# Two passes over the channels for the first four tiles of the first projection, with its modulation loaded in channel halves

## The chip, the cores and the metric

The kernel runs on one core of a Trainium2 chip. The metric is the device time of one execution in microseconds (us). All data are 32-bit floats. The engines of the core run their own instruction streams in order and meet at semaphores: TensorE (products and transposes into PSUM), VectorE, ScalarE and GpSimd (element work; GpSimd here mostly issues loads and stores), and SyncE, which only issues transfers. "Channels" are the 1024 columns of the model, in eight blocks of 128.

## The reference, cut to what matters

Two model blocks are computed one after the other on 1024 tokens of x and 256 context tokens. The change touches only the beginning, the modulated norm and the first product of the first layer:

```python
def _modulate(x, c, norm_g, w_ada, b_ada):      # its meaning, written short
    shift, scale, gate = split(silu(c) @ w_ada + b_ada, 3)   # 1024 columns each
    h = rmsnorm(x, norm_g) * (1 + scale) + shift
    return h, gate

h, gate = _modulate(x, c, ...)
hc, gate_c = _modulate(xc, c_ctx, ...)          # the context has its own condition
q, k, v, ... = _split(h @ w_in, ...)            # then rotation (rope) of q and k, attention, ...
```

The first 512 columns of `w_in` make the queries of the window attention; they are rotated and kept transposed. Everything behind that (attentions, a second layer, a state-space block, the embedding at the end) is not changed.

## The kernel before, in words

A planner in Python lays out the whole program as a list of stages. Every PSUM bank use is a numbered "fill" of a ring: `main` has banks 0 to 4, `turn` banks 5 and 6; bank 7 holds attention outputs later on. The writer of a fill waits until the bank's last fill was drained, the reader waits until the fill is full. Then each engine's program is written by one walk over the stages, so the order of work on each engine is this walk's order, and an engine that waits holds all that stands behind it.

The start of the program, before the change:

- SyncE (L850 to L865) loads, in this order, four chunks of the modulation weights (`ev_w_ada`, 512 columns each, 2 MB; chunks 0 and 1 are the shift, 2 and 3 the scale), the first projection weights (512 columns of `ev_w_in`, 2 MB), the rotation tables, the window mask, and the next projection's weights (1 MB).
- GpSimd (L882) loads tiles of x and the context (128 tokens, 0.5 MB) into three slots. From the fourth tile on it waits until a normed tile has left its slot: `gp.wait_ge(s_xn, j["xn"] - 2)`.
- ScalarE issues the small loads (L2249), makes the conditions, and then takes for each tile the sum of squares (L2188) and the inverse root (L2182, L2183).
- VectorE (L1858) multiplies each tile by its inverse root into one of seven slots of `RP`. After the fourth tile (`i == 3`) it does its part of the modulation: for each chunk a copy of the product out of PSUM (L1817) and, one chunk later, an addition of the bias (L1826), at the end the scale times the gain (L1833). After that come the even ones of the eight channel blocks of the first group of four tiles: the gain operation `hT = turned * scale + shift` (L1783). ScalarE does the odd ones (L2200) and waits for `s_mod` first.
- TensorE does all four chunks: `modulation` (L1208, sixteen instructions of products a chunk, four groups of rows side by side; L1218, eight small products that turn and sum them), then the transposes of the first group's eight blocks (L1135), then the first projection (L1318).

The first projection has ten tiles of 128 tokens. A tile is eight products of 128 x 512, issued as sixteen instructions, into one bank. Groups of normed tiles are turned between them: group 0 is tiles 0 to 3, group 1 tiles 4 to 7, group 2 the two context tiles 8 and 9. Group 1's eight blocks are turned after tiles 1 to 3 (three, three and two), group 2's after tiles 4 to 6. VectorE rotates a finished tile out of PSUM into one of three stage slots (`rope`: L1759, L1763, L1764, L1770), TensorE turns it (L1153) after the products of the following tile, and ScalarE copies it to `RQ` (L2237). `stage_free` makes VectorE wait until the tile three before was turned.

## Time and profile before

| what | value |
|---|---|
| median of 3 runs | 2816.3 us (2813.34 to 2818.73) |
| the profiled execution's own time | 2816.37 us |
| its span, first to last instruction | 2814.4 us |
| TensorE busy (products) | 2725.0 us, 97% of the span |
| VectorE, ScalarE, GpSimd busy | 1069.6, 785.2, 218.2 us |
| granted TensorE clock, mean | 0.994 of full |
| first projection product begins, last tile ends | 51.2 us, 139.0 us |

The profile is of one execution. Times in it are from the span's start. Line numbers (L1318) are those of the kernel before. "Wait before" of an instruction is the idle time of its engine ahead of it, with what released it. "psum<-RW,hT" names destination and sources by their buffers. PE is TensorE's products, PEld its weight loads, which may overlap products; DVE is VectorE, ACT ScalarE, POOL GpSimd, SP SyncE, and a q behind a name is that engine's issuing of transfers. Granted clock 1.00 is 2.4 GHz, 0.50 is 1.2 GHz.

### The profile page before, as it was taken

To read this page: it belongs to the slowest core of one execution; us is meant where nothing else is said; L and a number is where in the kernel's file an instruction comes from. 1 tells how busy PE (TensorE), PEld (TensorE's weight loads), DVE (VectorE), ACT (ScalarE), POOL (GpSimd) and SP (SyncE) were. 2 spreads that over 40 slices of the span, in tenths; PEclk is the share of its full clock that TensorE was granted. 3 is DMA by queue.
4 is the path that set the end of the run, shared out by engine and by line. 5 is a ranking of instruction groups with operands and counts; after the bars stand their busy time and mean duration, and the time that the engine had idled before them with its cause. 6 is when DMAs were issued, how large, how long until landed. Compare 5 with 4: busy or idle time off the path is not lost.

```text
span 2814.4 us, 32462 instructions
## 1 busy us (share of the span) xinstructions
PE 2725.0 (97%) x12154; PEld 1528.1 (54%) x12154; DVE 1069.6 (38%) x3023; ACT 785.2 (28%) x1684; POOL 218.2 (8%) x401
## 2 busy tenths in 40 slices
PE   5999999999999999999999999999999999999999
PEld 2477544477744445466655476444564465644444
DVE  3257521199811233344400075123744373412211
ACT  3136400177711112222200165112211363121100
POOL 2000000000000000000060030010000002011000
PEclk8999999999999999999999999999999999999999
DMA  7031000012012220211011101152220104125321
GB/s 262 4 104 41 20 30 30 30 68 72 20 53 74 90 86 27 94 38 38 12 34 40 40 24 39 64 97 90 108 102 30 68 17 133 68 92 185 131 75 49
DMA packets 73019, 188.46 MB, mean 67 GB/s; under 512 B 6972, under 2 KB 9728, under 8 KB 71936
## 3 DMA queue, kind: packets, MB, share of 16 engines
q0 software_dynamic: 26656, 94.84, 10.5%
q1 hardware_dynamic: 45456, 91.16, 9.4%
q8 instruction: 99, 1.62, 0.3%
q14 instruction: 56, 0.46, 0.1%
q10 hardware_dynamic: 752, 0.38, 0.0%
HBM read 143.69 MB, written 43.01 MB: 66 GB/s over the span
## 4 chain that ended last, share of the span: by engine, by line
PE 92%; DVE 3%; issue 2%; ACT 2%; DMA 1%; ACTq 0%; POOL 0%; DVEq 0%
PE psum L1318 32%; PE psum L1282 13%; PE psum L1354 11%; PE psum L1366 6%; PE psum L1297 5%; PE psum L1384 5%; PE psum L1450 4%; PE psum L1381 4%; PE psum L1518 4%; PE psum L1153 1%; PE psum L1503 1%; PE psum L1523 1%; PE psum L1135 1%; PE psum L1208 1%; PE psum L1488 1%
## 5 line engine op out<-in xcount | busy, mean ns | idle before, releaser
L1318 PE MATMUL psum<-RW,hT 128*128 128x512 f32 (+2 forms) x2208 | 923.8, 573 | 7.5 <-ACT hT L2200 4.7
L1318 PEld LDWEIGHTS psum<-RW,hT 128*128 128x128 f32 x2208 | 427.1, 197 | 433.2 <-issue 411.3
L1282 PE MATMUL psum<-RW,RQ 128*128 128x512 f32 x832 | 360.9, 592 | 1.1 <-ACT RQ L2237 1.1
L1354 PE MATMUL psum<-RQ 64*128 64x256 f32 (+5 forms) x1344 | 291.7, 492 | 2.3 <-DVE small L2041 1.5
L2390 ACT ACTIVATE RP<-RP,small 128x1280 f32<-128x1280 f32 (+11 forms) x274 | 251.9, 920 | 131.1 <-DVE small L2041 127.0
L2041 DVE CUSTOM_DVE_ANT_0 RP<-psum,small 128x512 f32<-128x512 f32 (+1 forms) x382 | 201.4, 573 | 178.5 <-PE psum L1354 89.7
L1282 PEld LDWEIGHTS psum<-RW,RQ 128*128 128x128 f32 x832 | 156.3, 190 | 189.3 <-issue 189.3
L1366 PE MATMUL psum<-ident,RP 128*128 128x128 f32 x1388 | 203.7, 281 | 9.8 <-DVE RP L2054 4.5
L2402 ACT ACTIVATE RP<-psum 128x512 f32<-128x512 f32 (+1 forms) x288 | 149.9, 521 | 192.2 <-PE psum L1366 180.4
L1366 PEld LDWEIGHTS psum<-ident,RP 128*128 128x128 f32 x1388 | 149.3, 141 | 81.7 <-issue 67.9
L1354 PEld LDWEIGHTS psum<-RQ 64*128 64x128 f32 (+1 forms) x1344 | 139.2, 186 | 90.4 <-issue 48.9
L1384 PE MATMUL psum<-RQ,RP 128*128 128x128 f32 x1312 | 159.8, 276 | 0.5 <-ACT YR L2412 0.5
L1384 PEld LDWEIGHTS psum<-RQ,RP 128*128 128x128 f32 x1312 | 152.1, 192 | 5.3 <-issue 4.6
L2054 DVE COPY RP<-psum 128x512 f32<-128x512 f32 (+1 forms) x160 | 109.2, 682 | 75.0 <-PE psum L1366 73.9
L1381 PE MATMUL psum<-RP,RQ 128*64 128x128 f32 x1856 | 124.3, 278 | 1.6 <-DVE RP L2054 1.5
L1297 PE MATMUL psum<-hT,RW 128*128 128x512 f32 (+1 forms) x320 | 123.8, 550 | 0.0
L1518 PE MATMUL psum<-RW,hT 128*128 128x512 f32 x256 | 114.2, 599 | 2.7 <-DMA RW<-in_w_ple_gate 2.7
L1381 PEld LDWEIGHTS psum<-RP,RQ 128*64 128x64 f32 x1856 | 99.3, 136 | 26.9 <-issue 26.5
L1450 PE MATMUL psum<-RW,hT 128*128 128x512 f32 x256 | 111.7, 594 | 0.0
L2188 ACT ACTIVATE RP<-RX 128x1024 f32<-128x1024 f32 x44 | 46.4, 1054 | 192.6 <-DVE small L1729 164.6
L1297 PEld LDWEIGHTS psum<-hT,RW 128*128 128x128 f32 x320 | 60.7, 190 | 62.8 <-issue 61.2
L2237 ACT ACTIVATE RQ<-psum 128x512 f32<-128x512 f32 (+1 forms) x53 | 29.4, 555 | 231.8 <-PE psum L1153 231.8
(320 smaller groups left out, 2282.1 us busy)
## 6 DMA issues: line engine op xcount, KB each, us to landing
RW<-in_w_in SPq DMA_DIRECT2D x7, 2048.0 KB, 7.9
RW<-in_ev_w_in SPq DMA_DIRECT2D x6, 2048.0 KB, 7.9
RW<-in_od_w_ada SPq DMA_DIRECT2D x6, 2048.0 KB, 8.0
RW<-in_od_w_in SPq DMA_DIRECT2D x5, 2048.0 KB, 7.9
RQ<-in_ev_w_ada SPq DMA_DIRECT2D x4, 2048.0 KB, 21.0
RX<-in_x POOLq DMA_DIRECT2D x16, 512.0 KB, 6.0
y_even<-YR POOLq DMA_DIRECT2D x20, 256.0 KB, 2.3
RP<-y_even POOLq DMA_DIRECT2D x20, 256.0 KB, 3.0
```

Of the source, the lines that this page charges most:

```text
L1282: last = pe.matmul(main.bank(f), yT[:, kk, :], w_buf(n)[:, kk, :], start=kk == 0, stop=kk == KC - 1)
L1297: last = pe.matmul(main.bank(e["m"])[:, 0:e["n"]], w_buf(n)[:, kk, e["c0"]:e["c0"] + P], src[:, kk, e["t0"]:e["t0"] + e["n"]], start=kk == ...
L1318: last = pe.matmul(main.bank(f)[:, 0:nc_], lhs_of(st["lhs"], j["t"], kk), w, start=kk == 0, stop=kk == kn - 1)
L1354: last = pe.matmul(main.bank(f)[:, 0:pc["w"]], q, kk[:, keys], start=i == 0, stop=i == len(u["qk"]) - 1)
L1366: last = pe.transpose(turn.bank(ch["f"])[:, i * P:(i + 1) * P], pair_slot(st, u, lane)[:, at:at + P], ident[:, :])
L1381: last = pe.matmul(bank_o[64 * lane:64 * lane + 64, 0:P], u["v"][:, kt, vc:vc + 64], p_t, start=first, stop=final)
L1384: last = pe.matmul(bank_o[:, P * lane:P * lane + P], p_t, u["v"][:, kt, vc:vc + P], start=first, stop=final)
L1450: last = pe.matmul(main.bank(e["m"]), lhs_of("h", e["t"], kk), w_buf(e["w"])[:, kk, :], start=kk == 0, stop=kk == KC - 1)
L1518: last = pe.matmul(main.bank(fg), hT3[:, kk, tok], w_buf(st["w"][c])[:, kk, :], start=kk == 0, stop=kk == KC - 1)
L2041: drained(main, dve.tensor_tensor_reduce(pair_slot(st, u, lane)[:, pc["at"]:pc["at"] + pc["w"]], main.bank(f)[:, 0:pc["w"]], add, -scale, ...
L2390: fn(pr, pr, ACT.Exp, bias=mins[:, at, lane, n - 1:n], scale=-1.0, accum_out=sums[:, at, lane:lane + 1]).then_inc(s_pexp, 1)
L2402: turn.consumed(fn(pair_turned(ch["c"])[:, 0:n], turn.bank(ch["f"])[:, 0:n], ACT.Copy), ch["f"])
```

## The change

1. The modulation weights load in the order of columns 0, 2, 1, 3: shift and scale of the lower 512 channels first, then those of the upper 512. The first projection's weights are loaded in two pieces of four channel blocks: the lower piece between the second and the third chunk, the upper piece behind the fourth.
2. A new ring `early` has bank 7 alone. Each chunk of modulation (`first_modulation`) uses it twice, for its products and for the turned sum, which now follows in the same call; its reader is VectorE in both.
3. x tile 3 is loaded into `gate[:, 0:1024]`, which is not yet in use, without waiting for a slot. Tile 4 of x waits for the fourth modulation chunk's weights to land.
4. TensorE does chunks 0 and 1, two turned blocks, then the products over channel blocks 0 to 3 of tiles 0 to 3 into four banks; chunk 2 comes after tile 1, chunk 3 after tile 3. Then the upper four blocks of tiles 0 to 3 are added. Turned blocks of group 0 stand between tile 0's products.
5. Group 1's blocks are turned four after tile 2 and four after tile 3. A rotated tile is turned later than before: tile 0 after tile 3, 1 after 4, 2 and 3 after 5, 4 and 5 after 6, 6 to 8 after 7 to 9 (before: each tile after the next one's products).
6. VectorE makes the scales in halves and norms tiles 4 to 7 after all of group 0; tile 8 after the rotation of tile 0, tile 9 after group 1's first four blocks. ScalarE takes the square sums of tiles 4 to 8 after group 0's blocks.

The core of the diff, on the planner's side and the engines' new functions:

```diff
-        for _ in range(5):
-            plan_ada_chunk(even_cols)
+        for j in (0, 2, 1, 3):
+            n = new_weights(kview(ada_w[:, j * 512:(j + 1) * 512]), KC, 512, slot=2 + j)
+            even_cols["w"].append(n)
+            even_cols["steps"].append({"n": n, "j": j, "fill": early.new("dve"), "turned": early.new("dve")})
         stages += [even_cols, plan_norm(with_ctx, 0, True)]
-        gs = stages[-1]["groups"]
-        turns_a = planned([(1, gs[1], 3), (2, gs[1], 3), (3, gs[1], 2), (4, gs[2], 3), (5, gs[2], 3), (6, gs[2], 2)])
+        first_norm, gs = stages[-1], stages[-1]["groups"]
+        def plan_first(src, tiles, dst):
+            n = new_weights(src, KC, 512)
+            r = {"kind": "rope", "w": n, "dst": dst, "turns": 4, "lhs": "h", "gain": None, "back": False}
+            jobs = planned([(2, gs[1], 4), (3, gs[1], 4), (4, gs[2], 3), (5, gs[2], 3), (6, gs[2], 2)])
+            now = {3: [0], 4: [1], 5: [2, 3], 6: [4, 5], 7: [6], 8: [7], 9: [8]}
+            r["tiles"] = [{"t": t, "m": main.new("dve"), "hook": None, "jobs": jobs.get(t, []), "now": now.get(t, []),
+                           "needs": {4: gs[1], 8: gs[2]}.get(t)} for t in tiles]
+            for j in r["tiles"]:
+                if j["t"] < 4:
+                    number_turns(j["jobs"])
+                for i in j["now"] + ([9] if j["t"] == 9 else []):
+                    r["tiles"][i]["f"] = turn.new("act")
+                    r["tiles"][i]["st"] = new_stage(r["tiles"][i]["f"])
+                if j["t"] >= 4:
+                    number_turns(j["jobs"])
+            weights[n]["last"] = r["tiles"][-1]["m"]
+            return r
...
+        first_proj = plan_first(kview(we[:, 0:512]), with_ctx, qaT)
+        stages += [first_proj,
...
+            return gate[:, 0:1024] if i == 3 else RX[:, (i % 3) * 1024:(i % 3 + 1) * 1024]
...
+                if n == even_cols["w"][2]:
+                    f = first_proj["w"]
+                    sp.dma_start(w_buf(f)[:, 0:4, :], weights[f]["src"][:, 0:4, :]).then_inc(s_half, 16)
+                if n == first_proj["w"]:
+                    sp.dma_start(w_buf(n)[:, 4:KC, :], w["src"][:, 4:KC, :]).then_inc(s_w[w["slot"]], 16)
+                else:
+                    sp.dma_start(w_buf(n), w["src"]).then_inc(s_w[w["slot"]], 16)
...
-                        if j["x"] >= 3:
+                        if t == 4:
+                            wait_weights(gp, even_cols["w"][3])
+                        if j["x"] > 3:
                             gp.wait_ge(s_xn, j["xn"] - 2)
...
+            def first_modulation(c):
+                step = even_cols["steps"][c]
+                n, f = step["n"], step["fill"]
+                wait_weights(pe, n)
+                main.wait_drained(pe, f_cond)
+                early.wait_free(pe, f)
+                for r in range(2):
+                    for g in range(4):
+                        kk = 4 * r + g
+                        last = pe.matmul(early.bank(f)[32 * g:32 * g + 32, :], cond3[:, kk, :], w_buf(n)[:, kk, :],
+                                         start=r == 0, stop=r == 1)
+                early.written(last)
+                early.wait_drained(pe, f)
+                f = step["turned"]
+                for b in range(4):
+                    last = pe.matmul(early.bank(f)[:, 2 * b:2 * b + 2], mod_part(c)[:, b * P:(b + 1) * P], select3[:, :, 0],
+                                     start=True, stop=True)
+                early.written(last)
+            def first_projection(st):
+                n = st["w"]
+                g0 = first_norm["groups"][0]
+                def products(j, ks):
+                    f = j["m"]
+                    for kk in ks:
+                        if j["t"] == 0:
+                            turn.wait_drained(pe, g0["fills"][kk])
+                        last = pe.matmul(main.bank(f), lhs_of("h", j["t"], kk), w_buf(n)[:, kk, :], start=kk == 0, stop=kk == KC - 1)
+                        if j["t"] == 0 and kk + 2 in ks:
+                            turn_groups([(g0, kk + 2)])
+                    return last
+                turn_groups([(g0, 0), (g0, 1)])
+                pe.wait_ge(s_half, 16)
+                for j in st["tiles"][:4]:
+                    main.wait_free(pe, j["m"])
+                    products(j, range(4))
+                    if j["t"] == 0:
+                        turn_groups([(g0, 4), (g0, 5)])
+                    if j["t"] == 1:
+                        first_modulation(2)
+                first_modulation(3)
+                wait_weights(pe, n)
+                for j in st["tiles"]:
+                    if j["t"] < 4:
+                        main.written(products(j, range(4, KC)))
+                        turn_groups(j["jobs"])
+                    else:
+                        if j["needs"]:
+                            wait_group(j["needs"])
+                        main.wait_free(pe, j["m"])
+                        main.written(products(j, range(KC)))
+                    for i in j["now"]:
+                        turn_stage(st, st["tiles"][i])
+                    if j["t"] >= 4:
+                        turn_groups(j["jobs"])
...
-                    for i, j in enumerate(st["tiles"]):
-                        dve.wait_ge(s_rstd, j["rq"] + 1)
-                        if j["xn"] >= 7:
-                            turn.wait_full(dve, xn_group[j["xn"] - 7])
-                        sig(ts(xn_slot(j["xn"]), x_slot(j["x"]), rstd[:, j["rq"] % 8, 0:1], None, ALU.mult), s_xn)
-                        if i == 3:
-
-                            for c in range(len(even_cols["steps"])):
-                                modulation(even_cols, c)
-                            normed_groups(st["jobs"])
+                    for j in st["tiles"][:4]:
+                        norm_tile(j)
+                    first_modulation(0)
+                    first_modulation(1)
+                    first_scales(0)
+                    normed_groups(st["jobs"][:4])
+                    first_modulation(2)
+                    first_modulation(3)
+                    first_scales(1)
+                    mark(s_mod)
+                    mods[0] += 1
+                    dve.wait_ge(s_mod, mods[0])
+                    normed_groups(st["jobs"][4:])
+                    for j in st["tiles"][4:8]:
+                        norm_tile(j)
...
+                elif st is first_proj:
+                    for j in st["tiles"]:
+                        f, t = j["m"], j["t"]
+                        if t == 3:
+                            normed_groups(j["jobs"])
+                        main.wait_full(dve, f)
+                        stage_free(j["st"])
+                        so = stage_slot(j["st"])
+                        if t < NT:
+                            sig(rope(main.bank(f), 8, so, t, f), s_stage)
+                        else:
+                            drained(main, dve.tensor_copy(so, main.bank(f)), f)
+                            mark(s_stage)
+                        if t == 0:
+                            norm_tile(first_norm["tiles"][8])
+                        if t != 3:
+                            normed_groups(j["jobs"])
+                        if t == 2:
+                            norm_tile(first_norm["tiles"][9])
...
+                    for j in st["tiles"][:4]:
+                        norm_tile(j)
+                    for half in range(2):
+                        act.wait_ge(s_scale, half + 1)
+                        normed_groups(st["jobs"][4 * half:4 * half + 4])
+                    for j in st["tiles"][4:9]:
+                        norm_tile(j)
+                elif st is first_proj:
+                    for j in st["tiles"]:
+                        if j["t"] < 4:
+                            normed_groups(j["jobs"])
+                        if j["t"] == 2:
+                            norm_tile(first_norm["tiles"][9])
+                        for i in j["now"]:
+                            turned(st, st["tiles"][i])
+                        if j["t"] >= 4:
+                            normed_groups(j["jobs"])
+                    unturned = (st, st["tiles"][-1])
```

## Rows read from the trace of the kernel before

**Rows 1.** The page: shares of the chain that ended last, by engine
```profile
PE 92%; DVE 3%; issue 2%; ACT 2%; DMA 1%; ACTq 0%; POOL 0%; DVEq 0%
```

**Rows 2.** The chain, 0 to 150 us: start, length, what held it
```profile
8.09 8.73 DMA YR<-in_ev_b_lambda
...
20.84 6.62 DMA RX<-in_x
...
29.98 0.61 DVE RS L1817
30.63 1.87 PE psum L1218 x8
32.49 3.57 PE psum L1208 x16
...
44.13 0.82 DVE hT L1783
45.00 0.92 PE psum L1135 x4
...
79.95 6.87 PE psum L1318 x16
```

**Rows 3.** DMA issues, 0 to 120 us; the last number is us to landing
```profile
RW<-in_ev_w_in SPq DMA_DIRECT2D x1, 2048.0 KB, 24.9
```

**Rows 4.** Timeline, TensorE and SyncE's queue: start, length (us), operation, wait before it
```profile
16.27 5.19 SPq L861 DMA_DIRECT2D RW<-in_ev_w_in  x1
...
19.81 0.15 PEld L1208 LDWEIGHTS psum<-RQ,cond 128*32 128x32 f32 x4 [1.05 <-DMA RQ<-in_ev_w_ada]
...
51.22 13.97 PE L1318 MATMUL psum<-RW,hT 128*128 128x512 f32 x32 [0.92 <-ACT hT L2200]
...
89.76 7.11 PE L1318 MATMUL psum<-RW,hT 128*128 128x512 f32 x16 [1.16 <-ACT hT L2200]
...
99.77 7.03 PE L1318 MATMUL psum<-RW,hT 128*128 128x512 f32 x16
...
108.66 7.03 PE L1318 MATMUL psum<-RW,hT 128*128 128x512 f32 x16
...
117.09 7.03 PE L1318 MATMUL psum<-RW,hT 128*128 128x512 f32 x16
...
124.39 7.03 PE L1318 MATMUL psum<-RW,hT 128*128 128x512 f32 x16
```

**Rows 5.** Windows: busy us of PE, PEld, DVE, ACT, POOL; granted clock; DMA
```profile
30.00:41.00 11.00, 10.37 (x48) 4.74 (x48) 2.20 (x5) 0.00 (x0) 0.53 (x1) 0.50 1.05 391
...
45.50:48.50 3.00, 2.95 (x14) 2.32 (x12) 1.35 (x2) 0.78 (x1) 0.00 (x0) 0.50 0.01 5
```

**Rows 6.** Timeline of VectorE: modulation end, norms of tiles, rotations
```profile
43.57 0.17 DVE L1826 TENSOR_TENSOR small<-psum,small 128x8 f32<-128x8 f32 x1 [0.72 <-PE psum L1218]
...
59.06 0.88 DVE L1858 TENSOR_SCALAR RP<-RX,small 128x1024 f32<-128x1024 f32 x1 [2.36 <-ACT small L2183]
...
64.94 0.69 DVE L1759 TENSOR_TENSOR RS<-psum,cos_t 128x512 f32<-128x512 f32 x1
...
69.11 0.80 DVE L1783 TENSOR_SCALAR hT<-psum,small 128x512 f32<-128x512 f32 x1
```

**Rows 7.** Timeline of ScalarE: square sums of x tiles
```profile
18.07 1.04 ACT L2188 ACTIVATE RP<-RX 128x1024 f32<-128x1024 f32 x1
...
19.67 1.04 ACT L2188 ACTIVATE RP<-RX 128x1024 f32<-128x1024 f32 x1
...
57.32 1.06 ACT L2188 ACTIVATE RP<-RX 128x1024 f32<-128x1024 f32 x1 [1.40 <-DMA RX<-in_x]
```

**Rows 8.** Timeline of GpSimd: the load of x tile 7
```profile
53.80 0.53 POOL L882 DMA_DIRECT2D RX<-in_x  x1 [23.00 <-DVE RP L1858]
```

**Rows 9.** Timeline of TensorE: later modulation products at the full clock
```profile
206.24 1.92 PE L1208 MATMUL psum<-RW,cond 128*32 128x512 f32 x16
...
613.13 1.05 PE L1218 MATMUL psum<-select,RS 128*128 128x2 f32 x8
```

More of the change, by code:

```diff
@@ L170, in build @@
         turn = Ring(psum, [5, 6], sem("turn_full"), {"act": sem("turn_read_act"), "dve": sem("turn_read_dve")})
+        early = Ring(psum, [7], sem("first_modulation_full"), {"dve": sem("first_modulation_read")})
         s_first = sem("conditions_loaded")
+        s_scale = sem("first_scales_ready")
+        s_half = sem("first_input_weights_half_loaded")
+        s_x3 = sem("x_row_tile3_loaded")
         s_rows = sem("vectors_loaded")
@@ L715, in x_slot, with wait_x @@
         def x_slot(i):
-            return RX[:, (i % 3) * 1024:(i % 3 + 1) * 1024]
+            return gate[:, 0:1024] if i == 3 else RX[:, (i % 3) * 1024:(i % 3 + 1) * 1024]
+        def wait_x(eng, i):
+            if i == 3:
+                eng.wait_ge(s_x3, 16)
+            else:
+                eng.wait_ge(s_x[i % 3], 16 * (i // 3 + 1) - (16 if i % 3 == 0 and i > 3 else 0))
         def stage_slot(i):
@@ L853, in _ @@
                 if w["before"] is not None:
-                    main.wait_full(sp, weights[w["before"]]["last"])
+                    (early if w["before"] in even_cols["w"] else main).wait_full(sp, weights[w["before"]]["last"])
                 if n == even_rows["w"][0]:
@@ L1235, in _ @@
                 if k == "ada":
-                    for c in range(len(st["steps"])):
-                        modulation(st, c)
+                    first_modulation(0)
+                    first_modulation(1)
                 elif k == "norm":
-                    turn_groups(st["jobs"])
+                    continue
+                elif st is first_proj:
+                    first_projection(st)
+                    unturned = (st, st["tiles"][-1])
+                    later += [(turn, j["f"]) for j in st["tiles"][-2:]] + [(main, st["tiles"][-1]["m"])]
                 elif k in ("gated", "final", "plain"):
@@ L1847, in modulation, with norm_tile, first_modulation, first_scales @@
                 dve.wait_ge(s_mod, mods[0])
+            def norm_tile(j):
+                dve.wait_ge(s_rstd, j["rq"] + 1)
+                if j["xn"] >= 7:
+                    turn.wait_full(dve, xn_group[j["xn"] - 7])
+                sig(ts(xn_slot(j["xn"]), x_slot(j["x"]), rstd[:, j["rq"] % 8, 0:1], None, ALU.mult), s_xn)
+            def first_modulation(c):
+                step = even_cols["steps"][c]
+                f, j = step["fill"], step["j"]
+                early.wait_full(dve, f)
+                drained(early, dve.tensor_copy(mod_part(c), early.bank(f)), f)
+                f = step["turned"]
+                early.wait_full(dve, f)
+                drained(early, tt(modc[:, 4 * j:4 * j + 4, :], early.bank(f)[:, 0:8].rearrange("p (b j) -> p b j", j=2),
+                                  bada[0][:, 4 * j:4 * j + 4].unsqueeze(2).broadcast_to([P, 4, 2]), ALU.add), f)
+            def first_scales(half):
+                fence()
+                ks = slice(4 * half, 4 * half + 4)
+                for j in range(2):
+                    last = stt(sclc[:, j, ks], modc[:, 8 + 4 * half:12 + 4 * half, j], 1.0, ngain[0][:, ks], ALU.add, ALU.mult)
+                sig(last, s_scale)
+                fence()
             y_g = [0]
@@ L1892, in _ @@
                         if c == 0:
-                            dve.wait_ge(s_x[j["x"] % 3], 16 * (j["x"] // 3 + 1))
+                            wait_x(dve, j["x"])
                         main.wait_full(dve, f)
@@ L2238, in turned, with norm_tile @@
                 turn.consumed(last, f)
+            def norm_tile(j):
+                wait_x(act, j["x"])
+                square_sum(x_slot(j["x"]), j["xn"], j["rq"])
+                inverse_rms(j["rq"], 1, 1.0 / D)
             sq_index = {}
@@ L2285, in _ @@
                 if k == "norm":
-                    for i, j in enumerate(st["tiles"]):
-                        act.wait_ge(s_x[j["x"] % 3], 16 * (j["x"] // 3 + 1))
-                        square_sum(x_slot(j["x"]), j["xn"], j["rq"])
-                        inverse_rms(j["rq"], 1, 1.0 / D)
-                        if i == 3:
-                            act.wait_ge(s_mod, 1)
-                            normed_groups(st["jobs"])
+                    for j in st["tiles"][:4]:
[5 more added lines that the diff above has]
+                        norm_tile(j)
+                elif st is first_proj:
+                    for j in st["tiles"]:
[7 more added lines that the diff above has]
+                            normed_groups(j["jobs"])
+                    unturned = (st, st["tiles"][-1])
                 elif k in ("gated", "final", "plain"):
```

10 lines of the change are left out of this document (5 added, 5 removed).

## The prediction

> **What bounds the kernel now.** The page comes first: TensorE carries 92% of the chain of waits [rows 1], so a saving counts only where TensorE waits or works late. Then the chain of the first 150 us [rows 2]: before 51 us it does not run on projection work at all. It goes over a slow constant load (until 16.8 us), a load of x that waited for a free slot (20.8 to 27.5), and then link by link over copy, eight small products and sixteen modulation products. The reader should see two things there. The load of x tile 3 is the only one that holds the modulation up: VectorE takes the modulation only after it has normed tile 3. And the first projection weights, issued at 16.3 us, landed 24.9 us later, at 41.2 [rows 3, 4], ten us ahead of their first use at 51.22 [rows 4]. From 51.22 on TensorE's own rows tell the rest: tile 4 begins at 89.76, tiles 5 to 8 at 99.77, 108.66, 117.09 and 124.39 [rows 4]. A tile is 6.87 us [rows 2] and one turn of a rotated tile 0.43 (7.30 from tile 7 to tile 8), so what is above that is turns of normed tiles and waits. Last the clock: granted 0.50 (1.2 of 2.4 GHz) from 30 to 41 us, behind a wait of 8 us and although TensorE was busy 10.4 of these 11 us, and 0.50 once more from 45.5 to 48.5 [rows 5].
>
> I follow one moment through the change: the start of tile 4, before at 89.76.
>
> **Start, and the first two modulation chunks.** Tile 3 of x gets a slot of its own (in gate) and loads at once, so the load of 6.6 us leaves the chain. ScalarE starts at 18.07 and takes 1.60 us a tile [rows 7]; 1.74 us after the start of a tile VectorE can norm it, for 0.75 [rows 6, 7]. Tile 3 is then normed at 18.07 + 3 x 1.60 + 1.74 + 0.75 = 25.4 instead of 29.98 [rows 2]. The constants that let ScalarE and TensorE begin came last at 16.8 [rows 2], on a queue that now shares with 0.5 MB more. I add 0.6 (bounds 0, if the order of packets does not change, and 2.2, a third of the x load of 6.6 us). So 26.0.
> Modulation now runs through one bank, so chunk 1 cannot multiply before VectorE has read chunk 0's turned values. Chunk 0's products, 3.57 from 16.8 on, lie under the norming. What is left: copy 0.65, small products 1.87, read 0.2, products 3.57, copy with its signals 0.8, small products 1.87 [rows 2], together 9.0: 35.0. The weights for it are no wait, since TensorE's weight load for the second chunk was released by its landing at 19.81 [rows 4]; with 0.5 MB more of x beside it, some 1.3 us later (as 2 MB took 5 to 6).
> Four transposes at the low clock, 0.92, and one gain operation, 0.82 [rows 2], put the first channel block at 36.8. Projection so begins 14.4 us earlier than 51.22. Its lower weight half is 1 MB behind two chunks and lands well before.
>
> **The two passes.** PE's work is not reduced, only cut: four half tiles are 4 x 3.43 = 13.7, four groups of transposes 1.8, and two modulation chunks stand between them. At the full clock the sixteen products are 1.85 (1.92 in the row, less its overlap) and the eight small ones 1.0 [rows 9], with a wait of 0.9 for VectorE's copy between them that nothing covers, because TensorE is in order: 3.8 a chunk, 7.5 for two. The clock is low at the start. The two low stretches of before that TensorE worked through lasted 3 us and 11 us [rows 5], which costs half of each, 1.5 to 5.5; I take 2.6, nearer to the short one, since 512-column products without a gap follow. Sum: 36.8 + 13.7 + 1.8 + 7.5 + 2.6 = 62.4. Call this moment X: the last modulation product.
>
> **After X, the part that decides.** VectorE adds the bias and makes the second scales (0.56 before, 43.57 to 44.13 [rows 2, 6], now with two more waits on itself: 0.9), then the gain operation 0.8: TensorE starts the upper pass at X + 1.75. Tile 0 with the turns of blocks 6 and 7 between its products ends at X + 6.2, tiles 1 and 2 at X + 9.6 and X + 13.05.
> Norming of tiles 4 to 7 is behind all this on both engines. ScalarE ends block 7 at X + 5.3 and starts x tile 4; VectorE norms it from X + 7.0; only then may GpSimd ask for x tile 7, whose slot is tile 4's (1.05 us after the norm began: its 0.75, and 0.3 that I allow for the signal). From issue to ScalarE's start were 3.52 (53.80 to 57.32 [rows 7, 8]), so X + 11.5, and tile 7 is normed at 11.5 + 1.74 + 0.75 = X + 14.0. TensorE waits there for 1 us: the next transposes need all four tiles.
> It turns blocks 0 and 1 of tiles 4 to 7, and there it stands. Two turn banks; block 2 needs block 0 drained; VectorE drains even blocks, and its order is norm 7, rotation of tile 0, norm of tile 8, rotations of tiles 1 and 2, and only then block 0. Two rotations in a row, from the first one's start to a gain operation, are 4.17 (64.94 to 69.11 [rows 6]). So 14.15 + 2.15 + 0.85 + 4.17 = X + 21.3, plus 0.8 for the block: X + 22.1, while TensorE had finished block 1 at X + 15.0. **This new wait of 7.1 us is the change's main cost.** Behind it on TensorE are the upper pass of tile 3, blocks 4 to 7 and tile 0's deferred turn.
> From X + 22.15: two groups of transposes 0.9, half a tile 3.43, blocks 4 to 7 with the bank waits 2.95 (four times 0.44, and twice 0.6 of a gain operation that the banks expose), tile 0's turn with its wait 1.05. After 7 us of idling I expect the clock low again, with the same bounds and the same value, 2.6. So 22.15 + 0.9 + 3.43 + 2.95 + 1.05 + 2.6 = 33.1, less 0.5 because waits for a gain operation overlap the slow transposes: X + 32.6 = 95.0, against 89.76: **+5.2**.
>
> **From tile 4 to the end of the projection.** The products are the same. After tile 4 the deferred turn comes as soon as before, but VectorE's rotation must wait for it to free a stage slot: +0.45. After tile 5 two rotated tiles are turned (0.43 more) and one more block with its bank wait: gap 2.6 against 108.66 - 99.77 - 6.87 = 2.0. After tile 6 2.05 against 1.56. Tiles 7 to 9 as before. Sum **+1.5**. All later stages keep their order, TensorE nearly fills them, and their weights are released by this projection's last tile, so I carry the shift to the end unchanged: +6.7 on the profiled execution's 2816.4, which is the median of the runs shown (2816.3): **2823 us**.
> No price: the extra descriptors on SyncE's queue (one more issue, on a queue that is free of work from there to the last tile), x tiles 4 to 6 loading after 34 instead of at 20 (used after X + 5), the tables, needed at X + 14. If that cover went, the first would delay weights that have ten us in hand.
>
> **Rivals.** (a) The clock falls at each modulation gap too. TensorE there does bursts of 1.85 and 1.0 with 0.9 idle; for it speaks that 45.5 to 48.5 was low soon after sixteen small products and short waits [rows 5], against it that the long low stretch stood behind a whole wait of 8 us, and the gaps here are 0.9. Two low stretches of 3.3 us cost 1.7 each: 2826.5.
> The Trainium skill, page "TensorE: Matmul & The Clock Gate", section "A second HAM failure mode: psum-queue depth-cycling", states that short idles between groups of products make the clock gate swing and that bursts then pay the re-throttling; by that rule rival (a) would hold. The trace agrees in part, with its 0.50 at 45.5 to 48.5.
> (b) The clock stays high wherever I let it fall (the early stretch shorter, none after the stall): -2.6 and up to -1: 2819.5. For the first, the short stretch of [rows 5]; against the second, the only wait of that length in these rows ended at 0.50.
> (c) Faster: VectorE is not late. If x tile 7 came so early, or the rotations lay so well beside the upper passes, that block 0 was drained as it was turned, the 7.1 us and the low clock behind them (2.6) and the 1 us at X + 14 fall away: tile 4 at 84.3, 2812.3. It decides at X + 15: only a VectorE that has done three rotations by then wins, and rotation 2 can't begin before tile 2 ends at X + 13.05. For more than 0.2% the waits ahead of X would have to shrink too; TensorE's bare work from 35 to tile 4 is 41 us, so 2804 is the floor.
> (d) The change does not start projection early, because the constants or chunks land late: each us there is one us at the end; 2 us more give 2825.
>
> **How the numbers follow.** 0.2%, 5.6 us, is about what can be told from no change. Forecast, 2820 to 2826: 0.45. (a) with (d), 2824 to 2831: 0.22. (b), 2816 to 2820: 0.23. (c), 2804 to 2813: 0.10. The range 2814 to 2830 leaves out (c) and the end of (a). Slower than 2821.9: two thirds of the forecast case and nearly all of (a), 0.52; faster than 2810.7: 0.06; the rest, 0.42, is no change.
>
> **What the profile after would show.** Right: projection products from about 37 us; modulation products between them at about 48 and 59; then TensorE idle some 7 us between two groups of transposes of RP, released by VectorE's hT, shortly before 85, and the clock 0.50 behind it; tile 4 at 93 to 97. Wrong: no idle of over 3 us there, or tile 4 before 89; or modulation chunks in the gap of 3.6 us each (rival a). What would make it wrong most easily is the position of X, into which four terms go that are only bounded.

## The result, and the profile after

The changed kernel takes 2825.4 us (median of 5 runs, 2823.8 to 2829.6), the kernel before 2814.4 (5 runs, 2813.3 to 2818.7): ratio 1.0039, with a 95% interval of 1.0028 to 1.0051, slower by 11 us. The profiled execution took 2823.8 us, its span is 2821.6, and 7.2 us of span lie between the two profiles.

TensorE's timeline of the changed kernel: start, length, line, operation, and in brackets the wait before. L1294 is the product line of the first projection, L1275 the modulation's products, L1281 its small products, L1174 the transposes of normed tiles. A row with x8 or x16 is that many instructions in a line; eight instructions of 512 columns are half a tile.

```profile
17.96 3.64 PE L1275 MATMUL psum<-RQ,cond 128*32 128x512 f32 x16 [4.17 <-DMA YR<-in_ev_b_lambda]
...
29.32 3.27 PE L1275 MATMUL psum<-RQ,cond 128*32 128x512 f32 x16 [0.35 <-DVE small L1966]
...
36.01 2.05 PE L1294 MATMUL psum<-RW,hT 128*128 128x512 f32 x2 [0.63 <-DVE hT L1885]
...
46.50 1.92 PE L1275 MATMUL psum<-RQ,cond 128*32 128x512 f32 x16
49.24 1.05 PE L1281 MATMUL psum<-select,RS 128*128 128x2 f32 x8 [0.81 <-DVE RS L1963]
...
59.93 1.05 PE L1281 MATMUL psum<-select,RS 128*128 128x2 f32 x8 [0.81 <-DVE RS L1963]
62.65 1.90 PE L1294 MATMUL psum<-RW,hT 128*128 128x512 f32 x2 [1.66 <-DVE hT L1885]
...
67.00 9.02 PE L1294 MATMUL psum<-RW,hT 128*128 128x512 f32 x20
76.87 1.09 PE L1174 MATMUL psum<-ident,RP 128*128 128x128 f32 x8 [0.84 <-DVE RP L1956]
84.97 1.97 PE L1174 MATMUL psum<-ident,RP 128*128 128x128 f32 x8 [7.01 <-DVE hT L1885]
86.73 5.28 PE L1294 MATMUL psum<-RW,hT 128*128 128x512 f32 x8
...
95.47 7.03 PE L1294 MATMUL psum<-RW,hT 128*128 128x512 f32 x16
...
105.62 0.44 PE L1174 MATMUL psum<-ident,RP 128*128 128x128 f32 x2 [1.55 <-DVE hT L1885]
...
146.26 3.62 PE L1420 MATMUL psum<-RW,hT 128*128 128x256 f32 x16
```

Read it against [rows 4]. Projection begins at 36.0 instead of 51.2. Modulation chunks 2 and 3 stand between the half tiles (their small products at 49.24 and 59.93), each with a wait of 0.81 in its middle. The row at 84.97 is the result in one line: TensorE had turned two blocks of group 1 by 77.96, and the next transposes waited 7.01 us for a VectorE operation that writes hT. Tile 4 begins at 95.47, against 89.76 in [rows 4], and the next projection (L1420) at 146.26, against 139.0 in the table ahead.

VectorE in that wait (L1956 norms a tile, L1861 begins a rotation, L1885 is the gain operation):

```profile
69.61 0.75 DVE L1956 TENSOR_SCALAR RP<-RX,small 128x1024 f32<-128x1024 f32 x1 [3.36 <-ACT small L2336]
...
75.92 0.89 DVE L1956 TENSOR_SCALAR RP<-RX,small 128x1024 f32<-128x1024 f32 x1 [2.36 <-ACT small L2336]
76.94 0.69 DVE L1861 TENSOR_TENSOR RS<-psum,cos_t 128x512 f32<-128x512 f32 x1
...
78.94 0.89 DVE L1956 TENSOR_SCALAR RP<-RX,small 128x1024 f32<-128x1024 f32 x1
79.93 0.69 DVE L1861 TENSOR_TENSOR RS<-psum,cos_t 128x512 f32<-128x512 f32 x1
...
82.11 0.69 DVE L1861 TENSOR_TENSOR RS<-psum,cos_t 128x512 f32<-128x512 f32 x1
...
84.11 0.80 DVE L1885 TENSOR_SCALAR hT<-psum,small 128x512 f32<-128x512 f32 x1
```

Norm of tile 7, rotation of tile 0, norm of tile 8, rotations of tiles 1 and 2, and at 84.11 block 0, which TensorE had turned at 77.

The granted clock of some stretches (the number ahead of the DMA's two):

```profile
26.00:32.00 6.00, 4.55 (x24) 2.45 (x24) 1.21 (x3) 0.00 (x0) 0.00 (x0) 0.50 1.05 387
44.00:62.00 18.00, 15.36 (x70) 6.43 (x69) 2.32 (x8) 0.51 (x1) 0.00 (x0) 1.00 0.06 19
62.00:66.00 4.00, 3.35 (x7) 1.78 (x8) 1.06 (x2) 0.27 (x1) 0.00 (x0) 0.60 0.00 0
84.00:90.00 6.00, 5.03 (x12) 3.11 (x13) 2.34 (x4) 2.31 (x5) 1.39 (x3) 0.50 0.09 11
```

The clock is at 0.50 as the second chunk is multiplied (26 to 32; the first one, at 17.96, took 3.64 us as well), at full level through both modulation gaps (44 to 62), low again as the upper pass begins, and low for six us behind the long wait, where half a tile takes 5.28 us instead of the 3.60 that the same eight instructions take at full level below.

### The profile page after: what moved, and what is told of

It is laid out like the page before. It is cut to its first block, busy times and chain, and to the rows that moved or that the text cites. A ratio compares the mean times of both kernels' runs of the same rounds, so it can differ in the third digit from the quotient of the medians.

```text
span 2821.6 us, 32467 instructions
## 1 busy us (share of the span) xinstructions
PE 2727.2 (97%) x12154; PEld 1529.0 (54%) x12154; DVE 1070.2 (38%) x3026; ACT 785.4 (28%) x1684; POOL 218.8 (8%) x401
## 4 chain that ended last, share of the span: by engine, by line
PE 92%; DVE 3%; issue 2%; ACT 2%; DMA 1%; ACTq 0%; POOL 0%; DVEq 0%
PE psum L1420 30%; PE psum L1384 13%; PE psum L1456 11%; PE psum L1468 6%; PE psum L1399 5%; PE psum L1486 5%; PE psum L1552 4%; PE psum L1483 4%; PE psum L1620 4%; PE psum L1294 2%; PE psum L1192 1%; PE psum L1605 1%; PE psum L1625 1%; PE psum L1174 1%; PE psum L1590 1%
## 5 line engine op out<-in xcount | busy, mean ns | idle before, releaser
L1420 PE MATMUL psum<-RW,hT 128*128 128x512 f32 (+2 forms) x2048 | 855.0, 573 | 5.4 <-ACT hT L2353 2.6
L1420 PEld LDWEIGHTS psum<-RW,hT 128*128 128x128 f32 x2048 | 398.0, 198 | 397.6 <-issue 377.0
```

Source lines behind the costliest of these rows:

```text
L1420: last = pe.matmul(main.bank(f)[:, 0:nc_], lhs_of(st["lhs"], j["t"], kk), w, start=kk == 0, stop=kk == kn - 1)
```

## The experiments

For each the start of tile 4 in its profile is compared, and the interval from the first product of the projection to tile 4, because the first product itself moves between executions of one kernel (36.0 in the profile above, 37.9 in the next one). The changed kernel has 59.5 us from the first product to tile 4, and 60.1 in its second profile: differences of half a us between single profiles mean nothing.

**The changed kernel again.** No edit.

> The changed kernel once more, unaltered. The profiled executions stood 7.4 us apart, the medians 11. If the forecast's terms are all there is, tile 4 begins at 95 to 96 us again and the median lies 7 to 8 us above before (ratio 1.0026). If something later in the program also costs, the ratio stays near 1.0039 and the shift between the two profiles grows behind the first projection.

2827.6 us, ratio 1.0041 (1.0028 to 1.0055): the ratio stays, as the second case of the expectation has it. Tile 4 begins at 97.95, 60.1 us behind the first product; the wait for the gain operation is 7.00. The start is 2 us later than in the first profile. Behind the projection 2.5 us more are lost: from the start of the next projection (146.26 and 148.75) to the end the first profile takes 2675.3 us and this one 2677.9. The two profiles part at 1130 to 1160, where the granted clock of the three stretches of 10 us is 0.83, 0.88 and 0.78 here and 0.94, 1.00 and 1.00 there. A low stretch near 2230 to 2244 stands in both profiles and tells nothing of their difference; more on it below. So the wait is a constant of the program, the clock is not.

**Blocks ahead of the rotations.**

```diff
                         f, t = j["m"], j["t"]
-                        if t == 3:
-                            normed_groups(j["jobs"])
+                        if t < 2:
+                            normed_groups(st["tiles"][t + 2]["jobs"])
                         main.wait_full(dve, f)
...
-                        if t != 3:
+                        if t > 3:
                             normed_groups(j["jobs"])
```

> VectorE takes the gain operations of group 1's first four blocks ahead of the rotation of tile 0 and those of the other four ahead of the rotation of tile 1. Theory A (VectorE's order makes the 7 us wait, and the low clock stands behind it): the wait of 7.0 us shrinks to under 1, no stretch at clock 0.50 between 80 and 91, tile 4 begins at 86 to 87 instead of 95.5, time 8 to 9 us below the changed kernel, 2816. Theory B (the two passes and the modulation gaps inside them cost, and TensorE would be held somewhere else): tile 4 begins no earlier than 92, time at most 3 us below the changed kernel.

```profile
80.75 1.26 PE L1174 MATMUL psum<-ident,RP 128*128 128x128 f32 x8 [0.54 <-DVE hT L1885]
81.84 3.60 PE L1294 MATMUL psum<-RW,hT 128*128 128x512 f32 x8
...
88.90 7.03 PE L1294 MATMUL psum<-RW,hT 128*128 128x512 f32 x16
```

The wait is 0.54, half a tile behind it 3.60, and tile 4 begins 50.8 us behind the first product: 8.6 us less than in the changed kernel. 2819.9 us, ratio 1.0017 (1.0008 to 1.0026), 5.5 us below the changed kernel's median. The local gain is as expected. The total falls short of it, where 8 to 9 us were expected: this profile has a low stretch at 99 to 108 (tile 5 takes 8.7 us) and starts 2 us late, but whether that is so in the other ten runs, no profile shows. The same 8.73 us for tile 5 stand in two more profiles below (the slot of its own, the spread modulation) and not in the rest.

**x tile 7 in a slot of its own.**

```diff
-            return gate[:, 0:1024] if i == 3 else RX[:, (i % 3) * 1024:(i % 3 + 1) * 1024]
+            if i in (3, 7):
+                return gate[:, 0:1024] if i == 3 else gate[:, 1024:2048]
+            return RX[:, (i % 3) * 1024:(i % 3 + 1) * 1024]
...
-                        if j["x"] > 3:
+                        if j["x"] > 3 and j["x"] != 7:
                             gp.wait_ge(s_xn, j["xn"] - 2)
```

> The changed kernel with x tile 7 in a slot of its own too, so that its load no longer waits for the norm of tile 4. Theory A (the order on VectorE makes the wait): the norm of tile 7 comes 1.5 us earlier, but then tile 8 is waited for, and the three rotations still stand ahead of block 0: the wait before block 2 stays at 7 to 7.5 us, tile 4 begins at 94.5 to 95, under 1 us gained. Rival (the late load of x tile 7 is the cause): the wait falls under 3 us.

```profile
77.67 1.04 PE L1179 MATMUL psum<-ident,RP 128*128 128x128 f32 x8
85.33 1.97 PE L1179 MATMUL psum<-ident,RP 128*128 128x128 f32 x8 [6.63 <-DVE hT L1890]
...
94.89 7.03 PE L1299 MATMUL psum<-RW,hT 128*128 128x512 f32 x16
```

The wait is still 6.63, a little less than the 7 to 7.5 expected. The late load of x tile 7 is not its cause. First product to tile 4 is 57.1 us, 2.3 less than in the changed kernel, where under 1 was expected: 0.8 of it is the wait at 76 that is gone, 1 us a shorter low stretch behind the long wait (half a tile in 4.33 instead of 5.28), 0.4 the wait itself. One execution, 2824.9 us.

**The kernel before with x tile 3 in its own slot, alone.**

```diff
-            return RX[:, (i % 3) * 1024:(i % 3 + 1) * 1024]
+            return gate[:, 0:1024] if i == 3 else RX[:, (i % 3) * 1024:(i % 3 + 1) * 1024]
...
-                        if j["x"] >= 3:
+                        if j["x"] > 3:
                             gp.wait_ge(s_xn, j["xn"] - 2)
```

> The kernel before with one part of the change alone: x tile 3 in a slot of its own. Theory (that load was the only thing that held the modulation): VectorE takes the modulation at about 26 to 27 us instead of 29.98, chunks and transposes follow, first product at 47 to 48 instead of 51.2, time 3 to 4 us below before. Rival (the loads of weights, later by 0.5 MB, take its place): first product within 1 us of 51.2, no gain.

```profile
27.17 1.22 PE L1226 MATMUL psum<-select,RS 128*128 128x2 f32 x8 [4.01 <-DVE RS L1825]
...
35.59 3.64 PE L1216 MATMUL psum<-RQ,cond 128*32 128x512 f32 x16 [2.90 <-DMA RQ<-in_ev_w_ada]
...
51.03 13.97 PE L1326 MATMUL psum<-RW,hT 128*128 128x512 f32 x32 [0.92 <-ACT hT L2208]
```

VectorE does take the modulation 3.5 us earlier (27.17 against 30.63 in [rows 2]), but then TensorE waits 2.90 us for a modulation chunk to land, and the first product comes at 51.03. 2816.4 us, ratio 1.0005 (0.9996 to 1.0014). The rival was right in the time, which gains nothing that the runs can tell, and in that behind the load of x tile 3 stood the fourth chunk, at 35.6. "Within 1 us of 51.2" holds only against the first profile of before, whose clock was higher: here it is 0.50 from 36 to 48. The third profile of before, below, has the same clock there and begins the fourth chunk at 37.78 and its first product at 53.20, so of the 3.5 us some 2.2 are left like with like. The changed kernel does not meet this wait: between 17.96 and 36.01 its TensorE waits for VectorE alone, since two chunks and half of the projection's weights are enough for it to begin.

**Norms of tiles 4 to 6 in the idle time.**

```diff
                     normed_groups(st["jobs"][:4])
+                    for j in st["tiles"][4:7]:
+                        norm_tile(j)
                     first_modulation(2)
...
-                    for j in st["tiles"][4:8]:
-                        norm_tile(j)
+                    norm_tile(st["tiles"][7])
```

The same on ScalarE, between the two halves of the scales.

> The changed kernel with the square sums and norms of x tiles 4 to 6 done right behind the first four gain operations, where ScalarE and VectorE are idle (41 to 61 us), so that x tile 7 is loaded early too; the rotations still stand ahead of block 0. Theory A: VectorE begins the rotations 6 us earlier, as soon as tile 0 is complete, the wait before block 2 shrinks from 7.0 to about 2.5 us (rotation 2 can only start when tile 2 is complete), tile 4 begins at 89 to 91, time 5 to 7 us below the changed kernel. If instead the order alone counts and not when VectorE starts, the wait stays at 7.

```profile
79.12 1.09 PE L1174 MATMUL psum<-ident,RP 128*128 128x128 f32 x8 [2.02 <-DVE hT L1885]
80.05 5.29 PE L1294 MATMUL psum<-RW,hT 128*128 128x512 f32 x8
...
88.80 7.03 PE L1294 MATMUL psum<-RW,hT 128*128 128x512 f32 x16
```

The wait is 2.02, where about 2.5 was expected; 52.6 us from the first product to tile 4, 6.8 less than in the changed kernel, though the half tile behind even this wait took 5.29. 2819.8 us, ratio 1.0015 (1.0006 to 1.0024).

**Both: early norms, and blocks 0 to 3 ahead of the rotation of tile 2.**

```diff
-                        if t == 3:
+                        if t in (2, 3):
                             normed_groups(j["jobs"])
...
-                        if t != 3:
+                        if t > 3:
                             normed_groups(j["jobs"])
```

> The early norms of x tiles 4 to 6, and in addition VectorE takes blocks 0 to 3 of group 1 ahead of the rotation of tile 2 and the other four ahead of that of tile 3. Theory A: the 2.0 us that were left of the wait and the low clock behind it go too, tile 4 begins at 85 to 86, 10 us ahead of the changed kernel; the next projection 3 us ahead of before.

```profile
78.07 1.09 PE L1174 MATMUL psum<-ident,RP 128*128 128x128 f32 x8 [0.47 <-DVE hT L1885]
78.99 3.60 PE L1294 MATMUL psum<-RW,hT 128*128 128x512 f32 x8
...
86.05 7.03 PE L1294 MATMUL psum<-RW,hT 128*128 128x512 f32 x16
```

Wait 0.47, no low clock behind it, 49.6 us to tile 4. The next projection begins at 136.84, 2.2 us ahead of the first profile of before (3 expected). 2815.5 us, ratio 1.0003 (0.9994 to 1.0013): the order on VectorE and ScalarE alone brings the changed kernel back to where before is.

**The modulation spread out, nothing else.**

```diff
                     if j["t"] == 0:
                         turn_groups([(g0, 4), (g0, 5)])
+                        first_modulation(2)
                     if j["t"] == 1:
-                        first_modulation(2)
-                first_modulation(3)
+                        first_turned(2)
+                        first_modulation(3)
+                    if j["t"] == 2:
+                        first_turned(3)
```

`first_turned` is the second half of `first_modulation`, called from there for chunks 0 and 1.

> The changed kernel with nothing moved on VectorE or ScalarE; only TensorE's modulation is spread out: products of chunk 2 after tile 0's lower half, their turn after tile 1, products of chunk 3 right behind, their turn after tile 2, so that copies and scales lie under products. Theory B's share: two waits of 0.8 us, the 1.7 us before the upper pass and the low clock at 62 to 66 go, 4.5 us in all, while the wait of 7 us stays: tile 4 at 90.5 to 91.5. If theory A were all, tile 4 would stay at 94 to 96.

```profile
54.00 3.70 PE L1300 MATMUL psum<-RW,hT 128*128 128x512 f32 x8
...
58.35 4.54 PE L1300 MATMUL psum<-RW,hT 128*128 128x512 f32 x10
...
82.24 1.97 PE L1174 MATMUL psum<-ident,RP 128*128 128x128 f32 x8 [7.03 <-DVE hT L1894]
...
92.11 7.03 PE L1300 MATMUL psum<-RW,hT 128*128 128x512 f32 x16
```

No wait over 0.4 us is left between the half tiles and before the upper pass, and no low clock there (tile 0's upper half runs on at 58.35). The wait for VectorE is 7.03, untouched. 54.2 us to tile 4: 5.3 less than in the changed kernel, where 4.5 was expected; 0.6 of it is a shorter low stretch behind the long wait (half a tile in 4.65 instead of 5.28). Tile 4's own time, 92.1, is above the 90.5 to 91.5 expected because this execution began its products at 38.0. 2821.3 us, ratio 1.0020 (1.0011 to 1.0029).

**All three together.** The edits of the last two.

> Early norms, blocks ahead of the rotations and the spread-out modulation together. Both shares add: tile 4 begins at 80 to 82 instead of 95.5 (before 89.8), next projection 7 to 8 us ahead of before, time 2806 to 2809, ratio to before 0.9975. If the shares cover the same time, tile 4 begins at 84 to 86 and the gain over before is 3 us.

```profile
72.56 1.10 PE L1174 MATMUL psum<-ident,RP 128*128 128x128 f32 x8 [0.47 <-DVE hT L1894]
...
80.55 7.03 PE L1300 MATMUL psum<-RW,hT 128*128 128x512 f32 x16
...
131.34 3.62 PE L1429 MATMUL psum<-RW,hT 128*128 128x256 f32 x16
```

The shares add: 44.4 us from the first product to tile 4 is 15.0 less than in the changed kernel, against a sum of 15.2 (9.9 from the early norms with the blocks ahead, 59.5 to 49.6, and 5.3 from the spread modulation). The next projection begins at 131.34, 7.7 us ahead of the first profile of before. 2811.9 us, ratio 0.9986 (0.9977 to 0.9994): faster, but by 2 us in the median and 4 by the ratio, where 2806 to 2809 us and a ratio of 0.9975 were expected. The profiled execution, 2809.96 us, was the second fastest of its eleven.

**The context tiles' blocks ahead of their rotations too.**

```diff
-                        if t in (2, 3):
+                        if t >= 2:
                             normed_groups(j["jobs"])
...
-                        if t > 3:
-                            normed_groups(j["jobs"])
```

> The version with everything together, and in addition VectorE takes the context tiles' blocks ahead of the rotations of tiles 4 to 6. Theory: the wait of 1.56 us after tile 4 (for a gain operation that stands behind a rotation) falls to 0.5, nothing else moves much: the next projection begins 1 to 1.5 us earlier than in that version (131.3), time 1 us below it.

```profile
83.06 7.03 PE L1300 MATMUL psum<-RW,hT 128*128 128x512 f32 x16
...
91.22 0.66 PE L1174 MATMUL psum<-ident,RP 128*128 128x128 f32 x4 [0.47 <-ACT RQ L2398]
91.72 7.03 PE L1300 MATMUL psum<-RW,hT 128*128 128x512 f32 x16
```

From tile 4 to tile 5 are 8.66 us (10.42 in the version before this one). This is the best version: 2809.2 us, ratio 0.9974 (0.9964 to 0.9984), in the median 5 us below the kernel before and 16 below the changed one. From the first product to the next projection are 94.2 us, 1.0 less than in the version before, as expected; that the median is 2.8 us lower, where 1 was expected, the two intervals, which overlap, don't bear out. The profiled execution took 2812.6, the slowest of its nine, with the first product at 37.9.

**The kernel before with 6.9 us of products that nobody reads.** It adds work and changes no order.

```diff
+                        if st is stages[2] and j["t"] == 3:
+                            for kk in range(kn):
+                                pe.matmul(psum[:, 7, 0:nc_], lhs_of("h", j["t"], kk), w_buf(n)[:, kk, :],
+                                          start=kk == 0, stop=kk == kn - 1)
```

> The kernel before with eight more products behind tile 3 of the first projection, into a bank that nobody reads: 6.9 us of pure shift at full clock, no order and no wait changed. In every altered kernel so far the ratio lies 2 to 4 us above what its profile shows at the end of the first projection. Theory S (the level of the clock in the sparse stages behind depends on when they come, so that any shift away from before costs some 3 us more): ratio 1.0034 to 1.0038. Theory T (a shift is worth itself, and the rest belongs to the changed code): ratio 1.0024.

2821.1 us, ratio 1.0021 (1.0013 to 1.0030). Theory T: 6.9 us cost 6 (by the ratio) to 7 us (in the median), the 1.0034 of theory S lies outside the interval, and a later start of what follows carries no price of its own.

**Two more profiles of the kernel before.** No edit.

> The kernel before once more, for a second profile. If the stretches at clock 0.50 behind the first projection are a matter of the single execution, this one has them at other places than the first (1130 to 1150 and 2670), or of another length, and none or one near 2230.

> The kernel before a third time. Its first profile had tile 4 at 89.8 us, its second at 86.7, because the clock rose 6 us earlier in the modulation. If the early one is the usual case, it is 86.7 here too and the time under 2815; if the two levels are equally common, either may show, and the median of before lies between.

The second profile of before, then the third (L1218 are the modulation's small products, and the 7.1 us rows start tile 4):

```profile
35.78 1.05 PE L1218 MATMUL psum<-select,RS 128*128 128x2 f32 x8
36.76 1.92 PE L1208 MATMUL psum<-RQ,cond 128*32 128x512 f32 x16
...
86.72 7.10 PE L1318 MATMUL psum<-RW,hT 128*128 128x512 f32 x16 [1.16 <-ACT hT L2200]
```

```profile
35.99 1.87 PE L1218 MATMUL psum<-select,RS 128*128 128x2 f32 x8
37.78 3.64 PE L1208 MATMUL psum<-RQ,cond 128*32 128x512 f32 x16
...
91.53 7.10 PE L1318 MATMUL psum<-RW,hT 128*128 128x512 f32 x16 [1.17 <-ACT hT L2200]
```

and the granted clock of the same six us in both:

```profile
36.00:42.00 6.00, 5.50 (x48) 3.81 (x47) 2.87 (x8) 0.41 (x1) 0.00 (x0) 1.00 1.05 384
```

```profile
36.00:42.00 6.00, 6.00 (x31) 3.00 (x28) 1.36 (x3) 0.00 (x0) 0.00 (x0) 0.50 1.06 386
```

One program, the same instructions, and tile 4 at 86.7, 89.8 (the first profile) or 91.5. The own times of the three executions are 2813.3, 2816.4 and 2818.1 us, in the same order and as far apart. Both expectations held in part. What differs most from one execution to the next is the start, and the early case is not the only usual one. Behind the projection the low stretches of the three stand mostly at the same places, against what was expected: each has one within 1130 to 1150 and within 2670 to 2690 (0.91 or 0.83 on the mean of 20 us), only the second has one at 1840 to 1860 (0.91), and none has one near 2230.

That last place is where the changed order differs. Before, then the changed kernel:

```profile
2220.00:2250.00 30.00, 25.57 (x194) 14.45 (x193) 20.40 (x83) 16.53 (x63) 1.09 (x2) 1.00 0.26 89
```

```profile
2220.00:2250.00 30.00, 27.06 (x144) 13.99 (x142) 15.01 (x66) 12.55 (x50) 0.55 (x1) 0.83 0.22 79
```

The granted clock of these 30 us is 1.00 in all five profiles with the order of before (the two with an edit too) and 0.83 to 0.94 in eight of the nine with the changed order; only the one with all three edits has 1.00. From one and the same VectorE instruction near 2220 to another near 2250 it is 29.3 us in each of the five and 30.3 to 31.7 in the eight, so 1 to 2.4 us are lost. Why the clock falls there was not tested. It is made up for elsewhere in most executions: from the start of the next projection to the end, eleven of the fourteen profiles take 2675.0 to 2675.5 us, whichever order they have, and three of the changed order more (2676.4 with all three edits, 2677.9 the changed kernel again, 2678.3 with the context tiles' blocks ahead).

## Why the prediction was right, and where its size was off

The direction, and the mechanism with its place, were right, and 2825.4 lies in the range. Step by step:

- **Start.** The products of the projection were to begin at 36.8 and began at 36.0. The constants came 1.1 us later than before (17.96 against 16.8), for which 0.6 was allowed; with x tile 3's slot as the only change they come at 18.02, and at 16.77 to 17.04 in the four profiles that load it as before, so its load is what delays them. In nine profiles with the changed start the first product stands at 36.0 to 36.5 four times and at 37.8 to 38.1 five times, and 36.8 lies between. That the load of x tile 3 was "the only one" that held the modulation up was wrong: taken alone, its removal leads to a wait of 2.9 us for the fourth chunk, and no gain in time that the runs can tell. The forecast for the changed kernel did not hang on this, since there the chunks come in another order.
- **The two passes.** X came at 61.0, forecast 62.4. A modulation chunk was 3.65 us (3.8), with the wait of 0.81 (0.9). Rival (a), the clock falling at each gap, held neither at the first gap nor, if one reads the stretch at 1.00 from 44 to 62, at the second one's products. But it fell at 62 to 66, behind the second gap and a wait of 1.66 us: the upper pass of tile 0 took 1.5 us more than my X + 6.2, and the half of the rival that stands there is real. It stands in all six profiles that keep these gaps: the first two products of the upper pass take 1.50 to 1.90 us there, and 1.0 at full level. The rule of the Trainium skill that the prediction names (page "TensorE: Matmul & The Clock Gate", section "A second HAM failure mode: psum-queue depth-cycling"), that short idles between bursts make the clock swing, fits the 0.60 at 62 to 66 and not the 1.00 before it. The spread modulation took waits and low clock away together, 5.3 us.
- **The wait that decides.** Forecast 7.1 us, from X + 15.0 to X + 22.1; measured 7.01, from X + 17.0 to X + 24.0, both ends 2 us later, 1.5 of it because tile 0's upper half was. Its cause is shown: with the gain operations ahead of the rotations it is 0.54, with the three rotations begun 6 us earlier 2.02, and with x tile 7 loaded early still 6.63.
- **Behind it.** The low clock was expected to cost 2.6; at 84 to 90 the granted clock is 0.50, and the half tile and the two groups of transposes there took 2.5 more than at full level. Tile 4 began at 95.5 (95.0). That it lies so near is in part luck: X came 1.4 us early and the upper pass was 2 us late, and in the second profile tile 4 stands at 97.95.
- **To the end of the projection.** +1.5 forecast, 1.55 measured (95.47 to 146.26 is 50.8, and 89.76 to 139.0 was 49.2). VectorE's late rotation shows as the wait of 1.55 at 105.62, against 1.06 before.
- **The sum.** Forecast +6.7; between the two profiles 7.4 in own time. The medians stand 11.0 apart. The term that was mis-sized is the reference: the sum was set against one execution of before, 2816.4, "which is the median of the runs shown". With five runs the median of before is 2814.4, 2.0 below (2814.1 to 2814.7 in the three sets of 19 or 27 runs beside the experiments), and the profiled execution of the changed kernel was the fastest of its five, 1.6 below its median: 7.4 + 2.0 + 1.6 = 11.0. The three profiles of before explain the 2.0 by the clock in the first 50 us: their own times differ as their tile 4 does. That the same makes the runs without a profile gather near 2813.5, 2816.3 and 2818.5 is inferred. For the changed kernel's own spread the two profiles show two places, the start (first product at 36.0 or 37.9) and 1130 to 1160, where the second one loses 3 us against the first. "I carry the shift to the end unchanged" held in the first profile (7.3 us at the next projection, 7.2 at the end) and not in the second (9.8 and 12.2).

For the same reason the versions' totals lie above what their profile shows against the first profile of before, whose tile 4 stands at 89.8 and not at the 86.7 of the quicker executions: 7.7 us ahead at the next projection gave 2 to 4 us. Measured from the first product, no version of the changed kernel lies more than 1.5 us off what was expected of it; the totals do.

## What to carry to other kernels

Where work is cut in passes to start TensorE early, write down each other engine's order over the same stretch: what stands ahead of the operation that frees a two-bank ring decides, not when TensorE is ready. Here the first product came 15 us earlier and tile 4 still 6 us later: 21 us were lost between them, part of them by three rotations ahead of one gain operation, late norms, and modulation turns that nothing covered. Moving the short operations ahead of the long ones and the norms into idle time brought back 10 of the 21, and spreading the modulation 5, without a single instruction less. A profile is one execution; where its start runs at half clock, compare intervals inside the stretch, and take the median of several runs as the reference of a sum of a few us.

## What the runs showed of the hardware

The clock's low stretches differ from one execution to the next of the same program: in the kernel before it was back at the full level at about 36, 42 or not before 48 us (in the first two it fell once more, to a mean of 0.72 and 0.77 at 42 to 48), and with it the own times were 3.1 and 4.9 us apart from the quickest. Modulation products at the low level take 3.6 us a chunk and 1.9 at the full one, so the busy row alone tells the level. After the wait of 7.0 us the clock was low for about 6 us in the changed kernel, and after one of 2.0 us the half tile behind it was as slow (5.29 against 5.28 us), while after 0.47 and 0.54 it was not (3.60): a wait did not have to be long to cost as much again behind it. Nor did its length alone decide: behind the waits of 1.88 and 1.95 us at 67 and 64 us in two profiles of before the clock stayed at 1.00 (64 to 72), behind the wait of 1.66 us ahead of the upper pass it fell in all six profiles that have it, and behind the one of 1.55 us ahead of tile 5 in three of eight.
